# Layer 0 of a two-layer decoder trunk: first gate before the second values, map scaling on GpSimd, two weight pieces split with an accumulating DMA

## What is computed

```python
def reference(x, c, norm_w, w_mod, b_mod, w_in, w_out, ...):
    for layer in range(2):
        shift, scale, gate = split(silu(c) @ w_mod[layer] + b_mod[layer], 3)
        hdn = rms_norm(x, norm_w[layer]) * (1 + scale) + shift
        q1, k1, v1, g1, q2, k2, v2, g2 = split(hdn @ w_in[layer], 8)   # 512 columns each
        if layer == 0:
            y1 = diff_attention(q1, k1, v1, ...)      # ends in rms_norm(o, subln)
            y2 = dilated_attention(q2, k2, v2, ...)
        else:
            y1 = moba_attention(q1, k1, v1, ...)
            y2 = stick_breaking_attention(q2, k2, v2)
        y = concatenate([y1 * silu(g1), y2 * silu(g2)]) @ w_out[layer]
        x = x + gate * y
    return x
```

## Time and profile before

| what | value |
|---|---|
| median of three runs | 324.62 us (324.25 to 324.77) |
| profiled execution | 324.23 us, span 322.4 us |
| busy | PE 299.4 us (93%), DVE 235.2, ACT 196.9, POOL 16.2 |
| granted clock of PE | 0.997 of full |
| span 110 to 130 us | PE 20.00 of 20, DVE 14.67, ACT 17.38, POOL 8.05 |
| span 130 to 150 us | PE 18.21 of 20, DVE 17.21, ACT 18.18, POOL 2.30 |
| span 150 to 242 us | PE 92.00 of 92, DVE 69.79, ACT 52.27; DMA share 0.55 |

### The profile page before, as it was taken

One profiled execution on the slowest core, in us unless ns is written; L12 is line 12 of the kernel. 1 busy time (PEld: TensorE's weight loads), 2 busy tenths in 40 slices (PEclk: granted clock), 3 DMA queues, 4 the chain that ended last, 5 costly groups with the idle time before them and its releaser, 6 DMA issues.

```text
span 322.4 us, 4790 instructions
## 1 busy us (share of the span) xinstructions
PE 299.4 (93%) x1709; PEld 237.6 (74%) x1709; DVE 235.2 (73%) x480; ACT 196.9 (61%) x401; POOL 16.2 (5%) x24
## 2 busy tenths in 40 slices
PE   3498998999998999989999999999999999899995
PEld 2476876777555688886576888888987799798783
DVE  3898999998886697698957457989773547638633
ACT  3625568736745687998256446556664798959400
POOL 0000000000000942020000000000000000000000
PEclk9999999999999999999999999999999999999998
DMA  7999999495678958688752315679547148000011
GB/s 253 363 401 411 405 406 399 147 328 180 248 265 255 332 203 317 216 329 320 260 196 65 133 65 195 209 256 305 209 155 277 48 143 273 23 0 2 0 67 65
DMA packets 19879, 70.31 MB, mean 218 GB/s; under 512 B 2192, under 2 KB 2576, under 8 KB 19856
## 3 DMA queue, kind: packets, MB, share of 16 engines
q1 hardware_dynamic: 19280, 67.91, 58.4%
q0 software_dynamic: 576, 2.10, 1.7%
HBM read 68.95 MB, written 1.05 MB: 217 GB/s over the span
## 4 chain that ended last, share of the span: by engine, by line
PE 68%; DVE 12%; ACT 9%; DMA 5%; issue 3%; SPq 1%; ACTq 0%; DVEq 0%
PE proj L1082 46%; PE score L1082 13%; DMA raw<-in_w 5%; PE mixed L1082 5%; DVE raw L771 4%; DVE w_lo L751 3%; PE turned L1127 2%; ACT w_hi L478 2%; PE turned L1109 2%; DVE y L946 1%; DVE gt L938 1%; DVE probs L1021 1%; ACT y L502 1%; ACT gt L627 1%; SPq L449 1%
## 5 line engine op out<-in xcount | busy, mean ns | idle before, releaser
L751 DVE TENSOR_TENSOR w_lo<-raw,w_hi 128x1024 fp32r<-128x1024 f32 x68 | 82.3, 1222 | 14.1 <-ACT w_hi L478 13.6
L478 ACT ACTIVATE w_hi<-raw 128x1024 fp32r<-128x1024 f32 x68 | 70.6, 1050 | 17.8 <-DMA raw<-in_w 16.7
L1082 PE MATMUL proj<-w_hi,hy_hi 128*128 128x512 f32 x144 | 60.0, 417 | 4.8 <-DVE hy_lo L805 4.4
L771 DVE CUSTOM_DVE_ANT_0 raw<-raw,c_rows 128x1024 f32<-128x1024 f32 x48 | 59.0, 1251 | 0.0
L1082 PE MATMUL proj<-w_lo,hy_hi 128*128 128x512 f32 x144 | 56.9, 395 | 0.0
L1082 PE MATMUL proj<-w_hi,hy_lo 128*128 128x512 f32 x144 | 56.8, 394 | 0.0
L1082 PE MATMUL proj<-hy_hi,w_hi 128*128 128x256 f32 x176 | 52.5, 298 | 0.0
L1082 PE MATMUL proj<-hy_lo,w_hi 128*128 128x256 f32 x176 | 49.7, 283 | 0.0
L1082 PE MATMUL proj<-hy_hi,w_lo 128*128 128x256 f32 x176 | 49.7, 283 | 0.0
L1082 PEld LDWEIGHTS proj<-w_hi,hy_hi 128*128 128x128 f32 x144 | 27.5, 191 | 13.0 <-issue 3.9
L1082 PEld LDWEIGHTS proj<-hy_hi,w_hi 128*128 128x128 f32 x176 | 33.6, 191 | 2.1 <-issue 2.1
(11 more groups left out here) (147 smaller groups left out, 439.8 us busy)
## 6 DMA issues: line engine op xcount, KB each, us to landing
raw<-in_w SPq DMA_DIRECT2D x76, 512.0 KB, 4.7
raw<-in_w_mod SPq DMA_DIRECT2D x48, 512.0 KB, 5.7
xs<-in_x SPq DMA_DIRECT2D x1, 1024.0 KB, 5.2
qT<-in_w POOLq DMA_DIRECT2D x2, 512.0 KB, 6.5
kT<-in_w POOLq DMA_DIRECT2D x2, 512.0 KB, 8.4
...
```

The lines of the kernel that those rows point to most:

```text
L478: nc.scalar.activation(w_hi[:, slot(n), :, :], raw_tile(("w", n)), ACT.Copy).then_inc(hi_done, 1)
L751: nc.vector.tensor_tensor(w_lo[:, slot(n), :, :], raw_tile(("w", n)), w_hi[:, slot(n), :, :], ALU.subtract).then_inc(lo_done, 1)
L771: nc.vector.tensor_tensor_reduce(out=tile, in0=tile, in1=c_rows[:, :], scale=1.0, scalar=0.0, op0=ALU.mult, op1=ALU.add, accum_out=col(V_M ...
L1082: return nc.tensor.matmul(o, a, b, start=start, stop=stop, skip_group_check=True)
```

## The change

Layer 0 alone is touched, and the whole lies between steps 34 and 66.

1. **Order of chunks.** G1 takes steps 40 to 47, V2 steps 48 to 55. RING gives V2 and G1 each other's banks.
2. **Pieces.** Pieces are numbered in order of use, so 20 to 23 are now G1 and 24 to 27 V2. 25 and 26 are no longer plain but SUMMED: ACT makes w_hi and then w_lo = -w_hi, and a DMA issued by GpSimd reads the piece again from memory and adds it to w_lo. All four G1 pieces are now plain (before: two), and no V2 piece is (before: four).
3. **Map scaling.** Pairs 4 and 5 (maps 8 to 11) are scaled by GpSimd between its biases, in two instructions a map. Pairs 6 and 7 stay with ACT.
4. **Gate of G1.** Its lags are now (2, 4, 11, 12, 14) with the product with y as a step of its own (`gate_mix`); before (2, 5, 6, 8). So Abs, Exp and Ln come at steps 47 and 48, after 46 and 47 are done (before 55 and 56).
5. **Turns.** Pair 4's maps are turned at steps 54 and 55 (before 50, 51), pair 5's at 56 and 57 (before 54, 55); their products with the values at 57 and 58. The subln turns stay at 52 and 53.
6. **Tables.** The output of pairs 0 to 3 lies in `val[:, 1]` instead of `gt`. EARLY, MOD_AT, and with them the order of loads, change.

```diff
-    out += [(c, p, s) for c in (K2, Q2, V2, G1) for p in range(4) for s in range(2)]
+    out += [(c, p, s) for c in ((K2, Q2, V2, G1) if layer else (K2, Q2, G1, V2)) for p in range(4) for s in range(2)]
...
-PLAIN = (18, 19, 20, 21, 22, 23, 25, 26, 34, 37, 38, 39)
+PLAIN = (18, 19, 20, 21, 22, 23, 34, 37, 38, 39)
+SUMMED = (25, 26)
+SUMMED_HI = (36, 37)
...
-EARLY = {24: 14, 27: 16, 28: 13, 29: 12, 30: 10, 31: 9, 32: 12, 33: 11, 35: 12, 36: 10,
+EARLY = {24: 14, 27: 12, 28: 11, 29: 11, 30: 9, 31: 9, 32: 13, 33: 12, 35: 12, 36: 10,
...
-    return (2, 5, 6, 8) if c == G1 else (2, 3, 3 if s else 5, 4 if s else 6)
+    if c == G1:
+        return (2, 5, 5, 6, 8) if layer else (2, 4, 11, 12, 14)
+    return (2, 3, 3, 5, 6) if s == 0 else (2, 3, 3, 3, 4)
...
-    return 6 if group(j) == 0 else 7
+    return 6 if group(j) == 0 else {4: 11, 5: 8}.get(j, 7)
...
+def turn_lag(j):
+    return {4: 8, 5: 6}.get(j, 4)
...
                 nc.scalar.activation(w_hi[:, slot(n), :, :], raw_tile(("w", n)), ACT.Copy).then_inc(hi_done, 1)
+                if n in SUMMED:
+                    act.wait_ge(hi_done, split_count(n))
+                    nc.scalar.activation(w_lo[:, slot(n), :, :], w_hi[:, slot(n), :, :], ACT.Copy,
+                                         scale=-1.0).then_inc(neg_ok, 1)
...
+            def scale_map(M):
+                pool.wait_ge(inv_ok, M - 7)
+                for tile, cs in enumerate((slice(0, P), slice(P, MAPW))):
+                    i = nc.gpsimd.tensor_scalar(probs[:, M % 4, cs], probs[:, M % 4, cs], stat[:, M % 4, 4 + tile:5 + tile],
+                                                0.0, ALU.mult, ALU.add)
+                i.then_inc(prob_ok, 1)
+            for i, n in enumerate(SUMMED):
+                pool.wait_ge(neg_ok, i + 1)
+                nc.gpsimd.dma_start(w_lo[:, slot(n), :, :], w[n].rearrange("p (k n) -> p k n", k=2),
+                                    accum_op=ALU.add).then_inc(summed_in[i], 16)
...
+                if M >= 12:
+                    scale_map(M - 4)
```

More of the change, by code:

```diff
@@ L86, in split_count, with lo_count @@
     return SPLIT.index(n) + 1
+def lo_count(n):
+    return sum(m not in SUMMED for m in SPLIT[:SPLIT.index(n) + 1])
 def done_at(layer, c, side):
@@ L134, in pieces_lo @@
 def pieces_lo(layer, g):
-    return [n for n in SPLIT if lo_at(n) == STEPS * layer + g]
-RING = [{K1: 0, Q1: 1, V1: 2, K2: 0, Q2: 1, V2: 0, G1: 1, G2: 0, O0: 1, O1: 2},
+    return [n for n in SPLIT if n not in SUMMED and lo_at(n) == STEPS * layer + g]
+RING = [{K1: 0, Q1: 1, V1: 2, K2: 0, Q2: 1, V2: 1, G1: 0, G2: 0, O0: 1, O1: 2},
         {K1: 0, Q1: 1, V1: 0, K2: 1, Q2: 0, V2: 1, G1: 0, G2: 1, O0: 0, O1: 2}]
@@ L179 @@
               + [(1, GATE, k) for k in range(KB)])
-MOD_AT = [25, 26, 28, 29, 30, 33, 35, 37, 38, 41, 42, 43, 45, 46, 50, 51, 53, 57, 58, 59, 61, 63, 66, 68] + [STEPS + 16 + 3 * i for i in range(8)]
+MOD_AT = [25, 26, 28, 29, 30, 33, 35, 37, 38, 41, 42, 43, 45, 46, 50, 54, 55, 57, 58, 59, 61, 63, 66, 68] + [STEPS + 16 + 3 * i for i in range(8)]
 GATE_ROWS = (42, STEPS + 56)
@@ L236, in turned_at @@
     out += [("probs", j, 1) for j in pairs_at(layer, g, 4) if group(j) == 0]
-    out += [("probs", j, o) for o in range(2) for j in pairs_at(layer, g, 4 + o) if group(j)]
+    out += [("probs", j, o) for o in range(2) for j in range(4, PAIRS) if PAIR_AT[j] + turn_lag(j) + o == STEPS * layer + g]
     out += [("x", t) for t in range(2) if X_AT[t] == STEPS * layer + g]
@@ L396, in program @@
         dve_step = sem("dve_step")
+        neg_ok = sem("neg_ok")
+        summed_in = [sem(f"summed_in{i}") for i in range(len(SUMMED))]
         held_in = [sem(f"held_in{i}") for i in range(len(HELD))]
@@ L445, in _ @@
                             wait_step(sp, LAST[n])
+                        elif n in SUMMED:
+                            sp.wait_ge(hi_done, split_count(n))
                         else:
[L447 removed]
+                            sp.wait_ge(lo_done, lo_count(n))
                 whence = w_mod[mods.index(key[1])] if key[0] == "mod" else w[key[1]]
@@ L709, in _ @@
                             act.wait_ge(ms_ok, PARTS[3])
-                            nc.scalar.activation(sq[:, :, :], gt[:, :, :], ACT.Square, scale=P ** -0.5).then_inc(sq_ok, 1)
+                            nc.scalar.activation(sq[:, :, :], y_flat.rearrange("p (a b) -> p a b", a=2), ACT.Square, scale=P ** -0.5).then_inc(sq_ok, 1)
                         if c == "subln" and at == SUBLN_AT[0] - 4:
@@ L715, in _ @@
                             n = 4 * layer + 2 * (c - G1) + s
-                            if done_at(layer, c, s) + gate_lags(c, s)[0] == at:
+                            if done_at(layer, c, s) + gate_lags(layer, c, s)[0] == at:
                                 act.wait_ge(g_sig, n + 1)
                                 nc.scalar.activation(gt[:, s, :], gt[:, s, :], ACT.Exp).then_inc(g_gate, 1)
-                            if in_parts(layer, c) and done_at(layer, c, s) + gate_lags(c, s)[2] == at:
+                            if in_parts(layer, c) and done_at(layer, c, s) + gate_lags(layer, c, s)[3] == at:
                                 act.wait_ge(y_ok, n + 1)
@@ L938, in gate_product, with gate_mix @@
                 nc.vector.tensor_tensor(g, b[:, :], g, ALU.mult).then_inc(free_dve, 1)
+            def gate_mix(layer, c, s):
+                n, blk, g, _, ys = gate_of(layer, c, s)
                 if layer == 0 and c == G1:
@@ L1030, in _ @@
                         for s in range(2):
-                            sig, product, _, low = gate_lags(c, s)
+                            sig, product, gated, _, low = gate_lags(layer, c, s)
                             if done_at(layer, c, s) + sig == at:
@@ L1271, in project @@
                         wait_raw(pe, ("w", n))
+                    elif n in SUMMED:
+                        pe.wait_ge(summed_in[SUMMED.index(n)], 16)
                     else:
-                        pe.wait_ge(lo_done, split_count(n))
+                        pe.wait_ge(lo_done, lo_count(n))
                 if p == 0:
```

15 lines of the change are left out of this document (10 added, 5 removed).

## The result

The changed kernel takes 334.7 us (median of 4 runs, 333.5 to 336.1) against 324.67 us for the kernel before (four runs, 324.25 to 324.77; the 324.62 above is the median of three of them): a ratio of 1.0315, with a 95% interval of 1.0291 to 1.0338. It is slower, as forecast, but by 10.0 us instead of 4.6, and 3.1 us above the end of the range. The profiled execution took 334.09 us, its span is 332.3 us.

A forecast was written before the change was run, and what follows sets the result against it. PE, busy 93% at full clock, was taken as the bound. From 324.23 us: -2.0 PE work, -1.8 old waits, +1.9 kT copy, +6.7 subln turn, +0.3 pair 5's turn, so +5.1, or 329.3; range 325.4 to 331.6.

The forecast's parts named there:

- the load wait: Up to step 52: no separate wait for a load in the sum; Q2's last piece at step 38 lay under 1.9.
- the clock: Whole kernel: PE taken to be at full clock; the sum had no term for a slower one.
- PE's own work: G1 and V2 steps: eight G1 steps (13.1 us) become eight V2 steps at 1.39 (11.1), so -2.0 us.
- what PE waits for at the subln turns: Step 53: PE's second subln turn waits 6.7 us for ACT's copy of the first half, held behind pair 5's exponentials.
- t = 0: Start of pair 4's first exponential on ACT, forecast at 111.35 us; the count to the subln copy starts there.
- Rivals 1, 2 and 4: 1: DVE doesn't hold ACT up, 325.4, 0.08; 2: moved gate passes absorbed, 321.3, 0.07; 4: waits only move, 324.4, 0.04.
- place 1: K2's second turn: hi and negated copies of pieces 25 and 26 delay ACT's kT copy; PE waits 1.9 us.
- the end: After step 53: 0.3 us wait at pair 5's first turn, none at pairs 6 and 7; step 64's shift reaches the end.
- GpSimd's scaling: Maps 8 to 11, ahead of steps 54 to 57: 0.6 to 2.1 us a map, hidden at either end.
- the 0.4 us: DVE's norm scaling ahead of the subln turn: waiting for a GpSimd instruction would make the sum up to 0.4 higher.
- rival 3: Slower: piece 20 or 21 late for steps 40 or 42, or GpSimd stretches DVE's row block (0.5): 331.3, chance 0.10.
- so nothing up to there: Steps 50 and 52: accumulating DMAs land by 111 us even at five times a load's 4.3, before needed, costing nothing.

The follow-up runs named there:

- f1_pool: Kernel before, with only the map scaling of pairs 4 and 5 put on GpSimd and their turns and products later: 326.46 us.
- e4_g1late: Changed kernel, with ACT taking G1's two gate sides at steps 53 and 54 instead of 47 and 48: 331.71 us.
- e2_plain_dma: Changed kernel, with GpSimd's two DMAs writing w_lo plainly instead of adding to it, same bytes: 332.54 us.
- k3_hold: Kernel before, with three extra, unread copies on ACT ahead of its copy of the first subln turn, so PE waits at step 53: 330.27 us.
- k3_again: The kernel of k3_hold measured once more, in rounds against the kernel before: four times from 327.25 to 330.47 us, ratio 1.0136.
- e3_late: Changed kernel, with pieces 25 and 26 split at steps 38 and 42 instead of 36 and 37, and loaded later: 334.83 us.
- m1_turns: Kernel before, with pair 3's second map turned one step earlier and pairs 6 and 7 one step later: 324.33 us, ratio 0.9990.

## Why the prediction was right and where it was wrong

The profiled execution is 4.8 us above the forecast of 329.3. Three terms of the sum make that up: the load wait, put at nothing (2.4), the clock, which had no term (1.7), and PE's own work, mis-sized (0.7). The waits for ACT came as forecast.

**Right: what PE waits for at the subln turns.** The sum was made by following ACT and DVE in order from pair 4's first exponential. ACT's timeline of the changed kernel (it answers to the earlier trace rows):

```profile
83.61 1.04 ACT L502 ACTIVATE w_hi<-raw 128x1024 fp32r<-128x1024 f32 x1
84.68 1.06 ACT L505 ACTIVATE w_lo<-w_hi 128x1024 fp32r<-128x1024 f32 x1
85.65 0.67 ACT L565 ACTIVATE kT<-turned,v 128x512 f32<-128x512 f32 x1
...
114.25 0.40 ACT L609 ACTIVATE probs<-logits,stat 128x128 f32<-128x128 f32 x1 [1.69 <-DVE stat L883]
...
120.58 0.28 ACT L491 ACTIVATE n_y<-n_ms,v 128x8 f32<-128x8 f32 x1
...
123.78 0.63 ACT L748 ACTIVATE gt<-gt 128x512 f32<-128x512 f32 x1 [1.92 <-DVE gt L961]
...
128.36 0.40 ACT L609 ACTIVATE probs<-logits,stat 128x128 f32<-128x128 f32 x1 [2.05 <-DVE stat L883]
...
131.07 0.67 ACT L570 ACTIVATE y<-turned,v 128x512 f32<-128x512 f32 x1
```

From 114.25 to the copy at 131.07 are 16.8 us, forecast 16.7; both waits of ACT are there, 1.92 and 2.05, forecast as nearly 2 each. The steps between agree too: the seeds begin at 120.58, which is t = 6.33 (6.35), and DVE's scaling at 121.92, t = 7.67 (7.6). So this isn't two mistakes that cancel. t = 0 came at 114.25 instead of 111.35, 2.9 later, which is the load wait and some tenths; PE was late by the same (125.2 at the turn instead of 122.2), so the wait itself, 6.65, wasn't changed by it. Rivals 1, 2 and 4 needed ACT to be earlier and are out.

**Right: place 1.** The negated copy took 1.06 us beside the hi's 1.04; ACT's kT copy began at 85.65 (forecast 85.5), PE waited 1.73 (1.9).

**Right: the end.** The map turns of pairs 6 and 7 don't wait, pair 5's first waits 0.22, and the lateness that step 64 had (9.94 at the second mark of the ledger) reached the end unchanged (9.86).

**Right: GpSimd's scaling is hidden, though it is slow.** GpSimd's timeline, changed kernel (two instructions of a map each in the rows of L1104, and two of its other instructions), and two of DVE's, a row block and the norm scaling:

```profile
110.41 1.66 POOL L1120 TENSOR_TENSOR qn<-qn,cst 128x256 f32<-128x256 f32 x1
...
120.56 0.83 POOL L1104 TENSOR_SCALAR probs<-probs,stat 128x128 f32<-128x128 f32 x2 [3.71 <-DVE stat L898]
...
121.96 1.78 POOL L1120 TENSOR_TENSOR qn<-qn,cst 128x256 f32<-128x256 f32 x1
...
130.88 1.72 POOL L1104 TENSOR_SCALAR probs<-probs,stat 128x128 f32<-128x128 f32 x2 [1.25 <-DVE stat L898]
```

```profile
111.40 1.75 DVE L801 CUSTOM_DVE_ANT_0 raw<-raw,c_rows 128x1024 f32<-128x1024 f32 x1
...
121.92 1.22 DVE L1040 TENSOR_TENSOR val<-val,n_t 128x1024 f32<-128x1024 f32 x1
```

A map takes 0.83 us in the quick case and 1.72 beside DVE's w_lo, within the 0.6 to 2.1 of the prediction (in f1_pool and e4_g1late some took 2.8 to 2.9). The addition at 121.96 took 1.78, where the same one took 0.73 at 113.50; DVE's scaling, begun 0.04 us ahead of it, took its usual 1.22. So the 0.4 us that would have come by the rule of the Trainium skill ("SBUF — State Buffer", "Who interferes with whom") did not. As to which side is held up the trace agrees with it here: the later of the two was GpSimd's. The other order occurs as well: DVE's row block at 111.40 began while the addition of 110.41 was still under way, and took 1.75 us instead of 1.22. That is the 0.5 which rival 3 feared within the chain. It fell ahead of the chain: the row block in it, at 126.54, took 1.22.

**Wrong: "so nothing up to there" for the accumulating DMAs.** That step looked only at when the DMAs themselves must have landed. They did land in time, 9.9 us after issue, within the "five times the 4.3 us" that it allowed. What they took was the DMA engines' time from the loads beside them. The chain that ended last in the changed kernel goes through it (start, length, what):

```profile
88.43 1.14 DVE raw L801
...
89.60 9.42 DMA raw<-in_w
```

Piece 21's load starts when DVE frees its row block, takes 9.4 us instead of 4.4, and PE waits 2.41 at step 42. Rival 3 had named the mechanism and, as one of two, the piece and the step, at "about 1 to 2 us"; that it takes the adding, and not only the extra bytes, is what e2_plain_dma showed. The mistake there was to treat it as instead of the forecast. A late load and a late ACT copy don't exclude each other; they add. With it in the sum the time is 329.3 + 2.4 = 331.7.

**Wrong: full clock throughout.** No term of the sum had a clock. The trace of before gave no ground for that: its longest wait after 76 us is 0.9 us, so it didn't show what a wait of 6.7 does there, and the cost had to be bounded from both sides. A price for the slow level did stand in it, in a stretch that the prediction didn't read. Before, behind PE's waits of 3.7 and 2.2 us near the start:

```profile
18.12 0.63 PE L1082 MATMUL proj<-w_hi,hy_hi 128*128 128x512 f32 x1
...
20.45 0.40 PE L1082 MATMUL proj<-w_hi,hy_hi 128*128 128x512 f32 x1
```

The granted clock reads 1.00 for this stretch, and yet the matmuls took 0.63 and then 0.40 us, the same two lengths as at 133 and 137 us in the changed kernel. Whether the clock had fallen behind those waits or had not yet risen, the trace doesn't tell. In the changed kernel, behind the 6.65 us, PE worked at the 1.2 GHz level for 3.6 us: +1.7, which gives 333.4.

**Mis-sized: PE's own work, -2.0.** It came to -1.3. The 1.39 us of a split step on 512 columns is the pace of an unbroken row of them. Cut up by turns and scores, V2's steps took 1.43 each in twos (120.37 to 123.23) and 1.47 alone (136.72 to 138.19); over eight steps that is, by this estimate, about 0.5 of the 0.7. With it, 334.1; the small rest (kT 1.73 and not 1.9, pair 5's turn, 0.3 at K2's turns) goes either way by a tenth or two. The other three runs of the changed kernel took 333.47, 335.31 and 336.11 us, with clocks over the span of 0.985, 0.985 and 0.980 against 0.990 in the profiled one; where they differ isn't shown, since they have no trace.

**What stays open.** Why the same wait is followed by a low clock in one execution and not in another (2.63 us with it in k3_hold and without in k3_again; 2.41 in the changed kernel without, 1.96 in e4_g1late and 1.99 in e3_late with). And that m1_turns' later turns for pairs 6 and 7 cost what the earlier one gained was read from its waits only; ACT's order there wasn't varied further.
